# Two orders on ScalarE, the recurrent layer's output banks and layer 1's convolution taps in a one-core float32 kernel of four blocks

## The reference

```python
def rglru_mixer(x, w_in, conv_w, conv_b, gate_w, gate_b, a_param, w_out):
    y_br, x_br = jnp.split(x @ w_in, 2, axis=-1)
    y_br = jax.nn.gelu(y_br)
    xc = causal_dwconv(x_br, conv_w, conv_b)
    g = jax.nn.sigmoid(einsum('bsnc,gncd->gbsnd', blocks of xc, gate_w) + gate_b)
    log_a = -LRU_C * r_gate * jax.nn.softplus(-a_param)
    a, mult = jnp.exp(log_a), jnp.sqrt(-jnp.expm1(2.0 * log_a))
    bterm = mult * i_gate * xc
    h = scan(a, bterm)                       # h_t = a_t h_(t-1) + b_t
    return (h * y_br) @ w_out

def compress(t, pos, w1, b1, w2):            # NSA, keys and values
    blk = (t[:, :, tok_idx] + pos).reshape(...)   # 15 blocks of 32 tokens, every 16
    return jax.nn.gelu(blk @ w1 + b1) @ w2
```

## Time and profile before

| | |
|---|---|
| median of 3 runs | 2083.74 us (2082.51 to 2085.2) |
| the profiled execution | 2097.18 us, its span 2095.4 us |
| mean granted TensorE clock | 0.979 of full speed |
| TensorE busy | 2001.6 us, 96% of the span |
| VectorE busy | 1510.9 us, 72% |
| ScalarE busy | 885.7 us, 42% |
| HBM traffic | 318.11 MB, 152 GB/s on average |

### The profile page before, as it was taken

How to read it: one execution, slowest core, us unless ns; L and a number is a source line. 1 busy time by engine, 2 the same in 40 slices (tenths; PEclk the granted TensorE clock), 3 DMA queues, 4 the chain that set the end, 5 groups by cost and what they waited for, 6 DMA issues and landing times.

```text
span 2095.4 us, 33684 instructions
## 1 busy us (share of the span) xinstructions
PE 2001.6 (96%) x12854; PEld 1763.1 (84%) x12854; DVE 1510.9 (72%) x2770; ACT 885.7 (42%) x1401; POOL 357.0 (17%) x354
## 2 busy tenths in 40 slices
PE   7899999989999999988999999999999998999998
PEld 6789999857999888745888878888888865999998
DVE  7668887796987679876787658575666876675554
ACT  5634444263444523376243332212214347644443
POOL 0003224002323600001100222201231000003223
PEclk9999999989999999999999999999999999999999
DMA  6355565504546422101444325454554310554552
GB/s 256 126 193 185 185 237 198 208 26 161 201 181 221 171 101 101 61 1 44 178 181 154 138 75 187 160 201 181 181 212 160 121 61 21 181 183 165 196 198 84
DMA packets 46989, 318.11 MB, mean 152 GB/s; under 512 B 5008, under 2 KB 8080, under 8 KB 9488
## 3 DMA queue, kind: packets, MB, share of 16 engines
q1 hardware_dynamic: 45568, 309.58, 40.6%
q0 software_dynamic: 1296, 6.82, 0.9%
HBM read 315.33 MB, written 1.05 MB: 151 GB/s over the span
## 4 chain that ended last, share of the span: by engine, by line
PE 84%; DVE 10%; ACT 4%; issue 1%; DMA 0%; POOL 0%; DVEq 0%; ACTq 0%; POOLq 0%
PE ps L664 82%; ACT arena L1196 3%; DVE arena L2016 2%; DVE w_lo L1594 2%; PE ps L913 2%; DVE small L1816 1%; DVE arena L1838 1%; DVE ps L1805 1%; ACT L1196 0%; ACT w_hi L1196 0%; DVE arena L1576 0%; DMA x<-x_in 0%; DVE arena L1883 0%; PE ps L1102 0%; PE ps L1095 0%
## 5 line engine op out<-in xcount | busy, mean ns | idle before, releaser
L664 PE MATMUL ps<-h_hi,w_hi 128*128 128x256 f32 (+2 forms) x2632 | 841.7, 320 | 23.0 <-DVE h_lo L1586 8.2
L664 PE MATMUL ps<-h_lo,w_hi 128*128 128x256 f32 (+2 forms) x2632 | 833.7, 317 | 0.0
L664 PE MATMUL ps<-h_hi,w_lo 128*128 128x256 f32 (+2 forms) x2632 | 833.2, 317 | 0.0
L1594 DVE TENSOR_TENSOR w_lo<-ring,w_hi 128x1024 fp32r<-128x1024 f32 x457 | 580.6, 1276 | 309.9 <-ACT w_hi L1196 309.0
L1196 ACT ACTIVATE w_hi<-ring 128x1024 fp32r<-128x1024 f32 x457 | 479.8, 1055 | 560.5 <-PE ps L664 516.5
L664 PEld LDWEIGHTS ps<-h_hi,w_hi 128*128 128x128 f32 (+1 forms) x2632 | 503.4, 191 | 62.3 <-issue 17.5
L664 PEld LDWEIGHTS ps<-h_lo,w_hi 128*128 128x128 f32 (+1 forms) x2632 | 501.2, 190 | 33.8
L664 PEld LDWEIGHTS ps<-h_hi,w_lo 128*128 128x128 f32 (+1 forms) x2632 | 500.7, 190 | 33.7
L1196 ACT ACTIVATE arena<-ps 128x512 f32<-128x512 f32 (+2 forms) x246 | 141.1, 579 | 352.3 <-PE ps L664 303.8
L664 PE MATMUL ps<-hid_hi,w_hi 128*128 128x256 f32 (+1 forms) x736 | 224.9, 306 | 0.0
L664 PE MATMUL ps<-hid_lo,w_hi 128*128 128x256 f32 (+1 forms) x736 | 224.9, 306 | 0.0
(11 more groups left out here) (194 smaller groups left out, 1941.5 us busy)
## 6 DMA issues: line engine op xcount, KB each, us to landing
ring<-wstream SPq DMA_DIRECT2D x290, 1024.0 KB, 4.8
arena<-c_in POOLq DMA_DIRECT2D x7, 512.0 KB, 4.5
arena<-rpb POOLq DMA_DIRECT2D x2, 1536.0 KB, 6.6
x<-x_in SPq DMA_DIRECT2D x2, 1024.0 KB, 12.1
out<-arena SPq DMA_DIRECT2D x8, 128.0 KB, 2.0
cst<-consts SPq DMA_DIRECT2D x1, 928.0 KB, 11.9
prm<-params SPq DMA_DIRECT2D x1, 580.0 KB, 10.6
ring<-wstream SPq DMA_DIRECT2D x1, 512.0 KB, 4.4
```

Of the source, the lines that this page charges most:

```text
L664: ins = nc.tensor.matmul(*a, **k)
L1594: V.tensor_tensor(w_lo[:, job % SPLITS, :], raw_job(job), w_hi[:, job % SPLITS, :].bitcast(F32), ALU.subtract).then_inc(weights_ready, 1)
```

## The change

1. **ScalarE, recurrent layer.** The sigmoids of blocks 0 to 3 move from after `lru_y(15)` to before `lru_y(12)`; those of blocks 4 and 5 now come before the last round. All 10 Sqrt run together, and the last four Gelu follow them (they stood after the eighth).
2. **VectorE, recurrent layer.** The product of input gate and `l_x` leaves `recurrence` and is done for all blocks ahead of it; all 10 `decay_square` come first.
3. **Output banks.** `lru_out` uses bank `(m + 6) % 8`. In its residual the addition of tile m comes ahead of the rest `scaled_lo` of tile m - 1.
4. **First attention.** The 32 `n_blk` instructions move from VectorE to ScalarE (Identity with a bias), eight behind each of the rounds of kv4 to kv7's turn, with a semaphore of their own, `blocks_ready`.
5. **Layer 1's taps.** `per_job` becomes `[1,1,1,1,3,2,0,1,0,0,3,3,3,3,3,3]`.

```diff
-    return ((m + 7) % 8, 0) if stage == "lru_out" else (m % 4, m // 4)
+    return ((m + 6) % 8, 0) if stage == "lru_out" else (m % 4, m // 4)
...
                 else:
+                    if j == KL + 2:
+                        for n in range(4):
+                            lru_sigmoid(n)
                     lru_y(j)
-            for n in range(4):
+            for n in range(4, 6):
                 lru_sigmoid(n)
             ahead("lru_in", 16)
-            for n in range(4, KL):
+            for n in range(6, KL):
                 lru_sigmoid(n)
...
             for n in range(KL):
-                if n == KL - 2:
-                    for j in range(16, 20):
-                        lru_y(j)
                 act.wait_ge(dve_tile_ready, tiles.next())
                 go(l_t[:, n, :], l_t[:, n, :], ACT.Sqrt).then_inc(act_tile_ready, 1)
+            for j in range(16, 20):
+                lru_y(j)
...
                 ahead("nsa_kv", g)
+                if g >= 4:
+                    kv = (g - 4) // 2
+                    for m in range(2 * kv, 2 * kv + 2):
+                        freed("nsa_kv", m, 0)
+                    for jj in range(g % 2 * 8, g % 2 * 8 + 8):
+                        o = n_blk[:, kv * HALF + jj, :].rearrange("p (g c) -> p g c", c=NCMP)
+                        i = n_kc[:, kv, :, 2 * jj:2 * jj + CMP_STRIDE * (NCMP - 1) + 1:CMP_STRIDE]
+                        ins = go(o, i, ACT.Identity, bias=par("cmp_pos", kv * HALF + jj))
+                    if g % 2:
+                        ins.then_inc(blocks_ready, 1)
...
-                    if gain and m:
+                    if gain and m and (stage != "lru_out" or m == KD):
                         scaled_lo(m - 1, gain)
...
                     V.tensor_tensor(x[:, m, 0:S], x[:, m, 0:S], acc[b][:, 0:S], ALU.add).then_inc(acc_free[b], 1)
+                    if m and stage == "lru_out":
+                        scaled_lo(m - 1, gain)
...
-            for j in range(KL + 2, 17):
+            for j in range(KL + 2, 16):
                 ahead("lru_in", j)
-
+            for n in range(4):
+                gated_input(n)
+            ahead("lru_in", 16)
+            for n in range(4, KL):
+                gated_input(n)
+            dve.wait_ge(dve_step, step.next(KL))
...
                 link(V.tensor_tensor(l_i[:, n, :], l_i[:, n, :], l_t[:, n, :], ALU.mult))
-                link(V.tensor_tensor(l_i[:, n, :], l_i[:, n, :], l_x[:, n, :], ALU.mult))
...
-            for n in range(KL - 2):
+            for n in range(KL):
                 decay_square(n)
-            for n in range(2):
-                recurrence(n)
-            for n in range(KL - 2, KL):
-                decay_square(n)
-            for n in range(2, KL):
+            for n in range(KL):
                 recurrence(n)
...
-                per_job = [...] if l == 0 else [1, 1, 1, 1, 3, 3, 1, 1, 0, 0, 2, 2, 2, 3, 3, 4]
+                per_job = [...] if l == 0 else [1, 1, 1, 1, 3, 2, 0, 1, 0, 0, 3, 3, 3, 3, 3, 3]
```

More of the change, by code:

```diff
@@ L461, in program @@
         ln_added = sem("ln_added")
+        blocks_ready = sem("blocks_ready")
         branch_rounded, branch_split = sem("branch_rounded"), sem("branch_split")
@@ L612, in _ @@
             pool.wait_ge(c_ready, 2)
-            pool.wait_ge(operand_ready, KL + 2)
+            pool.wait_ge(blocks_ready, 2)
             for s in range(2):
@@ L1000, in cmp_hidden @@
                 ins.then_inc(acc_full[m], 1)
-            pe.wait_ge(operand_ready, oper.next())
+            pe.wait_ge(blocks_ready, 1)
             cmp_hidden(0, 0)
@@ L1008, in _ @@
             score_pair(None, 1)
-            pe.wait_ge(operand_ready, oper.next())
+            pe.wait_ge(blocks_ready, 2)
             cmp_hidden(1, 0)
@@ L1876, in _ @@
             for kv in range(2):
-                dve.wait_ge(acc_free[2 * kv + 1], USED["nsa_kv"][2 * kv + 1] + 1)
-                for jj in range(HALF):
-                    if jj % 8 == 0:
-                        ahead("nsa_kv", 4 + 2 * kv + jj // 8)
-                    o = n_blk[:, kv * HALF + jj, :].rearrange("p (g c) -> p g c", c=NCMP)
-                    i = n_kc[:, kv, :, 2 * jj:2 * jj + CMP_STRIDE * (NCMP - 1) + 1:CMP_STRIDE]
-                    ins = V.tensor_scalar(o, i, par("cmp_pos", kv * HALF + jj), None, ALU.add)
-                ins.then_inc(operand_ready, 1)
+                for g in range(2):
+                    ahead("nsa_kv", 4 + 2 * kv + g)
                 for m in range(2 * kv, 2 * kv + 2):
@@ L1935, in cmp_scale @@
                                 con("cmp_mask", q * NCMP, NCMP).unsqueeze(1).broadcast_to([P, HEADS, NCMP]), ALU.mult).then_inc(operand_ready, 1)
-                dve.wait_ge(operand_ready, KL + 3 + q + 1)
+                dve.wait_ge(operand_ready, KL + 1 + q + 1)
             def cmp_values():
```

5 lines of the change are left out of this document (4 added, 1 removed).

## The result

The changed kernel takes 2070.32 us (median of 6 runs, 2067.62 to 2077.1), the kernel before, run beside it, 2083.59 us (2081.56 to 2085.2). The ratio is 0.9943, with a 95% interval from 0.9929 to 0.9956: 13.3 us less. Run again later beside two other kernels it took 2068.13 us, ratio 0.9933 (0.9918 to 0.9948). The forecast was 2068.5 us.

A forecast was written before the change was run, and what follows sets the result against it. TensorE was taken as the bound (84% of the closing chain), its idles and the half clock behind them priced. Terms 3.9 + 4.2 + 4.5 + 2.6 = 15.2 us off 2083.74 gave 2068.5 us, range 2065.0 to 2076.0.

The forecast's parts named there:

- Recurrent part: Recurrent layer up to the first FFN: ScalarE's order, banks and sums together save 3.9 us, between 1.9 and 6.8.
- Sigmoids' own share: Recurrent layer, ScalarE: with 8 of 20 sigmoids moved into an earlier idle, Exp and Tanh start 3.65 us earlier.
- banks, sums and rests: Recurrent output product: two more records before the Gelu wait, 2 x 0.23 us; first FFN job's 0.47 us wait goes.
- I take 0: Square root's table load, 1.28 us, moved before the first FFN's norm root: priced at 0, with 1.28 kept for the range.
- First attention: Before nsa_gate: 2.70 us of TensorE idle plus 1.75 for half clock, less 0.25: 4.2 us, between 0.8 and 4.45.
- I take the row with the overlap: First attention: a block on ScalarE costs some 0.21 us, from a 311 ns Gelu row with about 0.1 us overlap.
- The first rival: First attention: ScalarE becomes late, idle shrinks only to 1.9 us, perhaps with slow clock; 3.4 us lost, 2071.9 us, chance 0.13.
- the prediction's own signs: First attention: blocks at 0.2 to 0.24 us, nsa_gate idle at most 0.5 us; wrong if rounds exceed 3 us.
- ScalarE's lead of three jobs: First attention: reason against ScalarE becoming late, though it is filled to its full 2.83 us per job.
- Layer 1, first rotation: Before the third query tile's turn: idle of 3.14 us goes, half clock gives 1.5; 4.5 us (2.9 to 4.7).
- First scores: Layer 1, before the first scores: idle falls from 3.28 to 1.7 us, clock perhaps kept; 2.6 us (1.6 to 3.2).
- The second rival: Layer 1's idle only moves: TensorE waits in the key tiles, costing 3.2 us, 2071.7 us, chance 0.12.

## Why the prediction was right

**Recurrent part**: 3.9 us forecast, 4.17 and 4.19 measured. The product ended at 126.17 (126.2), the Gelus started at 89.88 (89.65), the wait behind four records ended at 90.31 (90.1). The Sigmoids' own share was taken nearly right: 3.65 us forecast, 3.42 measured. For the banks, sums and rests I counted 0.47 + 0.46 and took 0 for the moved table load; undone alone they are worth 1.45 (at a like clock), since without the sums' order that load stands on the path. So "I take 0" came true, but only together with the new order of the sums, which the prediction did not connect with it. And that two more square roots stand ahead of the Gelus, which I entered as 0.64 us against the gain, was measured at 0.3 to 0.6.

**First attention**: 4.2 us forecast, 1.12 of idle and 1.69 behind it measured, 2.8. The step that failed is "I take the row with the overlap": 0.21 us for a block, where the trace shows 0.290. The first rival, at a chance of 0.13, named what happened ("the strided read is slower", rounds late, idle 1.9; it is 1.58); the slow clock that it held possible did not come. By the prediction's own signs this part was wrong: rounds follow at 3.29 us where more than 3 was to tell against it, blocks at 0.290 where 0.2 to 0.24 was named, and `nsa_gate` has an idle of 1.58 us where 0.5 was the most. ScalarE's lead of three jobs, the argument against the rival, did not cover three rounds that were each 0.57 us too long.

**Layer 1, first rotation**: 4.5 us forecast; 3.14 of idle went and with it a stretch of 3.4 us at half clock (1.7), 4.8. **First scores**: 2.6 forecast; idle from 3.28 to 1.52 (1.7 was named), full clock behind it, 0.95 in the stretch that follows: 2.7. The full clock alone would give 1.7 there; but 9.4 us behind the first scores TensorE now waits 0.68 us for ScalarE's exponentials, an idle that neither the kernel before nor the one with the taps set back has. The prediction had taken 2.6 instead of 3.2 us with an eye to them. With the taps set back, both idles and both stretches were again as before. The second rival, worth 0.12, did not occur: the rests of VectorE behind the moved taps kept TensorE waiting nowhere.

**Sum**: 15.2 us forecast, 14.5 at the places of the change, 13.3 by the first comparison of medians and 14.8 by the second. The misses, 1.4 us too much for the first attention and 0.3, 0.3 and 0.1 too little for the others, lay inside their own bounds, but for the first rotation's 4.8 (bound 4.7). That the sum is nearer than its worst term is in part luck: the small misses went against the large one. What the prediction did not have is the noise of the profile it started from, 13.4 us above the median: its two slow FFNs alone are some 15 us.

## What to carry to other kernels

Move work to an engine with slack only after pricing the very access pattern: the row that was taken had the same shape but a dense read and was 0.08 us too cheap, and eight such blocks per round turned slack into 1.6 us of wait. Undo parts one by one: the parts here meet (a reordering paid for a table load that another reordering had brought), and one of them, the Gelus' place, was a loss that the whole hid. Compare stages between marks, not spans, where one profile carries up to 15 us that the edit did not cause.
